# Hybrid SSD / DeltaNet layer on one core: merge-gate units woven into the chunk loop in steps of six matmuls

## The chip, the cores and the metric

The kernel runs on one core of a Trainium2 chip. The metric is the device time of one execution in microseconds (us), lower is better. Three runs of the kernel before gave 2930.74, 2930.89 and 2931.74 us; their median is 2930.89 us.

## The reference

One layer on x of 1024 tokens by 1024 channels, all in float32. What matters for the change:

```python
h = rms_norm(x, g_mix_pre)
z, xbc, dt_raw, qkv, gate, b_raw, a_raw, m_gate = split(h @ w_in)      # m_gate: 2048 columns
y_ssm = mamba2_branch(z, xbc, dt_raw, ...)      # recurrence over chunks
y_gdn = gdn_branch(qkv, gate, b_raw, a_raw, ...)  # recurrence over chunks, a triangular solve in each
gate_ssm, gate_gdn = split(sigmoid(m_gate))
mixed = gate_ssm * (y_ssm @ w_br_ssm) + gate_gdn * (y_gdn @ w_br_gdn)
x = x + rms_norm(mixed @ w_out, g_mix_post)
# then a gated conv-MLP (4096 wide) and a gated input embedding
```

The merge gate m_gate depends on h alone, and it is first used after both branches.

## The kernel before, in words

All activations are kept transposed: 128 channels on the partitions, 1024 tokens along the free dimension. A matrix product is cut into *units* of 128 output channels. A unit has 8 *steps*, one for each block of 128 input channels, and a step is six matmuls: two halves of 512 tokens, by high weights times high activations, high weights times low activations, low weights times high activations (`pe_steps`, lines 407, 410 and 411). GpSimd splits each unit's weights into high and low parts in `split_unit` (lines 392 and 394); a split of unit u waits until the unit before it has begun on TensorE (`unit_begun`), since there are two slots. SyncE loads the raw weights of two units in one block of 1 MB (`load_block`, line 369), and a block waits for the splits of the block two before it. The products are accumulated in PSUM, read by ScalarE (sigmoid or silu) or VectorE, and written ("spilled") to DRAM.

The stages, in order of time in the profile:

1. The convolution inputs, 36 units, each followed by four VectorE instructions (to about 512 us).
2. Stage A: the 16 units of z and gate, two for each of eight 128-token chunks. Between their steps TensorE does the DeltaNet preparation of a chunk: sums of squares (line 1024), transposed v (1031), Gram matrices (1009), transposed k (1043). The prepared tensors go to DRAM (`sp_a_stores`, lines 1148 to 1156), through SyncE's one queue, which also loads the next chunk (`sp_a_loads`, 1136 and 1141). The positions in the 16 steps of a chunk are 4, 8, 13 and 16.
3. The 16 merge-gate units, one after another (to about 952 us). Beside them VectorE inverts all 32x32 diagonal blocks by 63 dependent instructions (`dve_substitute`, lines 1189 to 1196); ScalarE stores them (line 1205).
4. The mixer: a loop over eight chunks, written as functions of one chunk for each engine (`pe_mixer`, `dve_mixer`, `act_mixer`, `pool_mixer`, `sp_mixer`). Nothing of it is issued before `ready_to_mix` holds on each engine, which asks for everything of stages 2 and 3. TensorE's order in `main` (line 749): two products with the DeltaNet state (710, "ks" and "qs"), the product with the SSM state (761, "off"), v_new (710), the intra-chunk product of one group of heads (742, `diag`), two products with v_new (710), `diag` of the other group, the state update (782), and then transposes and the block inverse of the next chunk. The matrix `dec` of 16 heads is loaded by a broadcast DMA (line 607) once `diag` has read the old one twice, then GpSimd subtracts and masks (669, 671), ScalarE takes the exponential (842), and VectorE multiplies by the scores (`mix_scores`, 913), which the next `diag` needs. VectorE writes the DeltaNet output behind it (`ygdn`, 984), and "off" waits for that.
5. The tail: branch projections, output projection, MLP and embedding; it first loads y from DRAM (line 1305).

The order within each engine's queue is that of the Python code; engines meet only through semaphores. The loops over chunks and units are hardware loops (`Fori`).

SBUF: `act_hi` and `act_lo`, the split activations (64 KB per partition), share their region with the mixer's buffers, so they are gone once the mixer begins.

Of the kernel before, what the change touches and what calls it, by code (L numbers as in the profile page):

```python
# [8 lines left out]
P = 128  # L9
# [25 lines left out]
def hybrid_block_kernel(nc, x, p, g_mix_pre, w_in, conv_ssm_w, conv_ssm_b, ssm_dt_bias, ssm_a_log, ssm_d, ssm_norm_g,  # L35
# [98 lines left out]
    zt = sb("zt", [P, KD, P], f32, ph2)  # L134
    gt = sb("gt", [P, KD, P], f32, ph2)
    dec = sb("dec", [P, SSM_HEADS, P], f32, ph2)
    bs = sb("bs", [P, 2 * SSM_GROUPS, P], f32, ph2)
    xc = sb("xc", [P, SSM_HEADS, SSM_HEAD_DIM], f32, ph2)
    xcd = sb("xcd", [P, SSM_HEADS, SSM_HEAD_DIM], f32, ph2)
    rinv = sb("rinv", [P, GDN_HEADS, P], f32, ph2)  # L140
    xinv = sb("xinv", [P, GDN_HEADS, P], f32, ph2)
    rhs = sb("rhs", [P, GDN_HEADS, P], f32, ph2)
    vnew = sb("vnew", [P, GDN_HEADS, P], f32, ph2)
    qs = sb("qs", [P, GDN_HEADS, P], f32, ph2)
    osq = sb("osq", [P, GDN_HEADS, P], f32, ph2)
    orst = sb("orst", [P, GDN_HEADS], f32, ph2)
    s_ssm = sb("s_ssm", [P, SSM_HEADS, SSM_HEAD_DIM], f32, ph2)
    s_gdn = sb("s_gdn", [P, GDN_HEADS, P], f32, ph2)
    ysum = sb("ysum", [P, D_MODEL], f32, ph2)
    xd = sb("xd", [P, KD, P], f32, ph2)  # L150
    yssm = sb("yssm", [P, KD, P], f32, ph2)
    ysq = sb("ysq", [P, KD, P], f32, ph2)
    yrs = sb("yrs", [P, SSM_GROUPS, P], f32, ph2)
    ygdn = sb("ygdn", [P, KD, P], f32, ph2)
    ph2.close()
    ph12.close()

# [83 lines left out]
    blocks_in, sub_step, d_kept = sem("blocks_in"), sem("sub_step"), sem("d_kept")  # L241
# [26 lines left out]
    def branch_weights(which, n):  # L268
# [25 lines left out]
    O_A = O_QKV2 + 4  # L294
    O_MG = O_A + 32
    O_BRS = O_MG + MG_T
    U_BRS = 1 + N_SPILL

# [3 lines left out]
            ("gdn", COL_QKV + 20 * P, 4, J_V + 4, O_QKV2), ("silu", COL_Z, Z_T, J_Z, O_A),  # L302
            ("silu", COL_GATE, GATE_T, J_GATE, O_A), ("sigmoid", COL_MG, 8, J_MG, O_MG),
            ("sigmoid", COL_MG + 8 * P, 4, J_MG + 8, O_MG + 8), ("sigmoid", COL_MG + 12 * P, 4, J_MG + 12, O_MG + 12)]
# [5 lines left out]
    def a_chunk(j0, n):  # L310
        return (0 if j0 == J_Z else 4) + n // 2

    def a_use(j0, n, it):

        b = A_BUF + n % 2
        return b, it * 2 + (O_A // NBUF + a_chunk(j0, n))

    def a_after(eng, s, it, c, per, more):

        eng.wait_ge(s, it * (2 * per) + (c * per + more + 1))  # L320
# [232 lines left out]
    def tokens(c, d=0):  # L553
        return slice((c + d) * P, (c + d + 1) * P) if isinstance(c, int) else ds(c * P + d * P, P)

    def chunk(c, d=0):
        return slice(c + d, c + d + 1) if isinstance(c, int) else ds(c + d, 1)
# [1681 lines left out]
```

## Time and profile before

| | us |
|---|---|
| median of three runs | 2930.89 |
| the profiled execution's own time | 2931.96 |
| span of the profile in that execution | 2929.4 |
| TensorE busy | 2631.1 (90%) |
| VectorE busy | 1395.2 (48%) |
| GpSimd busy | 1042.7 (36%) |
| ScalarE busy | 530.4 (18%) |

The profile's page divides the span into 40 slices of 73.2 us; a digit is the busy share in tenths. TensorE's digits fall to 5 to 7 in slices 14 to 19, which is the mixer. Times below are in us from the start of the span. In a timeline row the first number is the start, the second the length, then engine, line of the kernel, operation, output and inputs; in brackets stands the idle time in front of it and who ended it.

### The profile page before, as it was taken

The numbers are of one execution on the slowest core, as the hardware profiler recorded it, in microseconds if no ns is written. First come the engines' busy times: TensorE is split into PE (matmuls) and PEld (weight loads), VectorE is DVE, ScalarE is ACT, GpSimd is POOL, SyncE is SP. The second block draws the span as 40 slices with busy tenths as digits, with TensorE's granted clock in tenths as the row PEclk, the third lists the DMA queues.
The fourth block names the chain that finished last, engine by engine and source line by source line (L and its number), as shares of the span: only waits on it lengthen the run. The fifth ranks groups of instructions, "written<-read, shape, count | busy, mean of one in ns | idle before, by whom it ended". The sixth has DMA issues, their size and how long they took to land. (4 is left out here: it accounts for less than half of the span.)

```text
span 2929.4 us, 30007 instructions
## 1 busy us (share of the span) xinstructions
PE 2631.1 (90%) x11984; PEld 2129.1 (73%) x11984; DVE 1395.2 (48%) x1093; ACT 530.4 (18%) x530; POOL 1042.7 (36%) x549
## 2 busy tenths in 40 slices
PE   4999999899999667656999879999999999999995
PEld 3788887677787556554777658888888888888774
DVE  0679776212430455654133574444454444444664
ACT  3200111455310112222001320000000000000332
POOL 1233432465332343341325543333333333333361
PEclk8999999999999788887999989999999999999998
DMA  5122221787623655643333221111111111111231
GB/s 177 66 92 79 101 101 63 206 281 250 217 93 115 159 143 149 173 121 115 110 120 134 99 86 56 43 49 52 43 45 55 43 50 51 43 49 66 79 108 58
DMA packets 275592, 303.21 MB, mean 104 GB/s; under 512 B 43645, under 2 KB 241610, under 8 KB 271434
## 3 DMA queue, kind: packets, MB, share of 16 engines
q1 hardware_dynamic: 243280, 246.08, 27.4%
q10 hardware_dynamic: 32250, 56.28, 5.2%
q8 instruction: 42, 0.69, 0.1%
q14 instruction: 20, 0.16, 0.0%
HBM read 215.82 MB, written 86.51 MB: 103 GB/s over the span
## 5 line engine op out<-in xcount | busy, mean ns | idle before, releaser
L407 PE MATMUL ps<-act_hi,w_hi 128*128 128x512 f32 x2320 | 925.3, 399 | 40.0 <-DVE act_lo L1749 16.4
L411 PE MATMUL ps<-act_hi,w_lo 128*128 128x512 f32 x2320 | 916.8, 395 | 0.0
L410 PE MATMUL ps<-act_lo,w_hi 128*128 128x512 f32 x2320 | 911.0, 393 | 0.0
L392 POOL TENSOR_SCALAR w_hi<-w_raw 128x1024 fp32r<-128x1024 f32 x219 | 248.0, 1133 | 1491.9 <-PE ps L407 689.0
L394 POOL TENSOR_TENSOR w_lo<-w_raw,w_hi 128x1024 fp32r<-128x1024 f32 x219 | 574.9, 2625 | 18.3
L407 PEld LDWEIGHTS ps<-act_hi,w_hi 128*128 128x128 f32 x2320 | 437.5, 189 | 146.1 <-issue 27.8
L410 PEld LDWEIGHTS ps<-act_lo,w_hi 128*128 128x128 f32 x2320 | 437.7, 189 | 102.9 <-issue 2.2
L411 PEld LDWEIGHTS ps<-act_hi,w_lo 128*128 128x128 f32 x2320 | 437.1, 188 | 102.9
L1422 PE MATMUL ps<-f_hi,w_hi 128*128 128x512 f32 x480 | 189.1, 394 | 0.0
L1426 PE MATMUL ps<-f_hi,w_lo 128*128 128x512 f32 x480 | 188.2, 392 | 0.0
L1852 DVE TENSOR_TENSOR tile<-ps,tile 128x1024 f32<-128x1024 f32 x112 | 135.7, 1221 | 107.9 <-PE ps L1426 106.5
L2196 DVE SCALAR_TENSOR_TENSOR ring_a<-xin,par,ring_a 128x1024 f32<-128x1024 f32 x108 | 181.0, 1676 | 12.5 <-DVE ring_a L2196 1.6
L1425 PE MATMUL ps<-f_lo,w_hi 128*128 128x512 f32 x480 | 186.2, 388 | 0.0
L1640 ACT ACTIVATE fa<-fa 128x1024 f32<-128x1024 f32 x32 | 33.9, 1061 | 699.7 <-DVE fa L1831 699.7
L1396 PE MATMUL ps<-act_hi,w_hi 128*128 128x512 f32 x320 | 133.3, 416 | 23.6 <-DVE act_lo L1781 9.3
L1839 DVE TENSOR_TENSOR ring<-ps,fa 128x1024 f32<-128x1024 f32 x32 | 39.2, 1225 | 205.1 <-PE ps L411 203.9
L1825 DVE COPY xin<-ps 128x1024 f32<-128x1024 f32 x32 | 39.2, 1225 | 203.0 <-PE ps L411 199.5
L1400 PE MATMUL ps<-act_hi,w_lo 128*128 128x512 f32 x320 | 129.4, 404 | 0.0
L1399 PE MATMUL ps<-act_lo,w_hi 128*128 128x512 f32 x320 | 128.9, 403 | 0.0
L761 PE MATMUL ps<-s_ssm,xbc 128*128 128x512 f32 x32 | 27.7, 1016 | 102.8 <-DVE ygdn L984 102.8
L1426 PEld LDWEIGHTS ps<-f_hi,w_lo 128*128 128x128 f32 x480 | 90.1, 188 | 21.1
L1425 PEld LDWEIGHTS ps<-f_lo,w_hi 128*128 128x128 f32 x480 | 90.1, 188 | 20.2
(266 smaller groups left out, 2869.0 us busy)
## 6 DMA issues: line engine op xcount, KB each, us to landing
w_raw<-in_w_in_dram SPq DMA_DIRECT2D x34, 1024.0 KB, 5.3
spill<-ring_b ACTq DMA_DIRECT2D x68, 512.0 KB, 2.6
w_raw<-in_w_ffn_gate_dram SPq DMA_DIRECT2D x17, 1024.0 KB, 5.3
w_raw<-in_w_ffn_up_dram SPq DMA_DIRECT2D x17, 1024.0 KB, 5.4
w_raw<-in_w_ffn_down_dram SPq DMA_DIRECT2D x16, 1024.0 KB, 4.9
qkv_a<-spill SPq DMA_DIRECT2D x8, 1536.0 KB, 6.8
dec_a<-cum_rows SPq DMA_DIRECT2D x16, 512.0 KB, 12.6
gdn_in<-hrow SPq DMA_DIRECT2D x8, 1024.0 KB, 14.6
```

The source lines that it names most:

```text
L392: nc.gpsimd.tensor_scalar(hi, raw, 1.0, 0.0, ALU.mult, ALU.add).then_inc(split_done, 1)
L394: nc.gpsimd.tensor_tensor(lo, raw, hi.bitcast(f32), ALU.subtract).then_inc(split_done, 1)
L407: first = nc.tensor.matmul(o, wh, mov[0][:, k, c], start=(k == 0), stop=False)
L410: nc.tensor.matmul(o, wh, mov[1][:, k, c], start=False, stop=False)
L411: last = nc.tensor.matmul(o, wl, mov[0][:, k, c], start=False, stop=(k == KD - 1))
L1396: first = nc.tensor.matmul(dst, wh, mov[0][:, k, in_half(half)], start=(k == 0), stop=False)
L1400: last = nc.tensor.matmul(dst, wl, mov[0][:, k, in_half(half)], start=False, stop=(k == KD - 1))
L1422: first = nc.tensor.matmul(dst, wh[:, k, n * P:(n + 1) * P], mov_hi[:, k, c], start=(k == 0), stop=False)
L1425: nc.tensor.matmul(dst, wh[:, k, n * P:(n + 1) * P], mov_lo[:, k, c], start=False, stop=False)
L1426: last = nc.tensor.matmul(dst, wl[:, k, n * P:(n + 1) * P], mov_hi[:, k, c], start=False, stop=(k == 1))
L1852: v.tensor_tensor(tile3[:, j, :], buf(b), tile3[:, j, :], ALU.add).then_inc(tile_free[b], 1)
L2196: v.scalar_tensor_tensor(out=ring_a[:, slot, :], in0=xin[:, slot, tap:tap + SEQ], scalar=col_of(wname, tap * nt + t0 + n), in1=ring_a[:, s ...
```

## The change

- `act_hi`, `act_lo` and `ring_b` now live through the mixer. Room for them comes from: the wide table `tmh`, of which 128 columns a chunk are copied into `tmc` before stage A; `vnew` is written into `rhs`, `ygdn` into `gt`, `xd` into `yssm`, `osq` and `ysq` into one `sqs`, `yrs` into `sqs`, `xcd` into a half of `ring_b`. The new waits follow from that.
- Of the 16 merge-gate units, 3 stay ahead of the mixer; 13 (104 steps) are issued by `gemm` in `pe_mixer`: 8 steps in front of the first chunk, 12 in each chunk. All 13 use PSUM buffer 0, so each must be evicted (`mg_evict`) before the next begins.
- In `main`, `diag(c, 1)` goes ahead of the two products with v_new; on VectorE `ygdn` goes ahead of `mix_scores`.
- `dve_substitute` is cut into two halves of 128 rows: the first in stage A, in three pieces in chunks 4 to 6, the second behind stage A. `ready_to_mix` no longer asks for the stored inverse; that is waited for where it is needed.
- Stage A's DeltaNet work goes to steps 12, 15, 18, 21 of chunk 0 and 22, 26, 29, 32 of chunk 1.
- The hardware loops over stage A and over the mixer's chunks become straight-line code.

```diff
+    MG_PLAIN = 3
+    MG_MIX = MG_T - MG_PLAIN
@@ ready_to_mix
-        for i in range(2):
-            eng.wait_ge(spilled[i], 16 * (N_SPILL // 2))
         a_ended(eng)
-        eng.wait_ge(kept_bk, 16 * NCH + 1)
-        eng.wait_ge(d_kept, 16 * 8)
+        (kept_qk, kept_bk, kept_d, kept_n of all chunks)
+    def inverse_kept(eng):
+        eng.wait_ge(d_kept, 2 * 16 * 8)
@@ sp_mixer
+        def load_g(c):
+            inverse_kept(sp)
+            after(sp, yg_kept, c * 16)
+        blocks_at = {0: 4, 2: 5, 3: 6, 4: 7, 6: 8, 7: 9}
+        for c in range(NCH):
+            load_g(c)
+            load_qk(c + 1); load_xbc(c + 1); load_bv(c + 1)
+            if c in blocks_at:
+                block_load(blocks_at[c])
+            load_dec(c + 1); load_kd(c + 1); load_mq(c + 1); load_z(c + 1)
+            load_inv(c + 2)
@@ pool_mixer
+        split_unit(pool, U_MG, 0)
+        (memset nt, dd); ready_to_mix(pool); (memset s_ssm, s_gdn)
+        split_unit(pool, U_MG, 1)
+        decays(0)
+        split_unit(pool, U_MG, 2)
+        mg_split(0); decayed_x(0); mg_split(1)
+        for c in range(NCH):
+            states(c); skip_x(c)
+            if c % 2 == 0:
+                mg_split(3 * (c // 2) + 2)
+            elif c < NCH - 1:
+                mg_split(3 * (c // 2) + 4)
+            if c < NCH - 1:
+                decays(c + 1); decayed_x(c + 1)
+            if c % 2 == 0:
+                mg_split(3 * (c // 2) + 3)
@@ pe_mixer
+        def gemm(steps):
+            for _ in range(steps):
+                w, k = at[0] // KD, at[0] % KD
+                if k == 0:
+                    pe.wait_ge(tile_free[0], used_ahead(O_MIX, 0) + w)
+                    pe.wait_ge(split_done, 2 * (U_MIX + w) + 2)
+                pe_steps(pe, U_MIX + w, 0, range(k, k + 1), mov)
+                at[0] += 1
@@ main(c): the order after, gemm(n) new
+  ks, qs, off, gemm(2), v_new, diag 0, gemm(2), diag 1, ds, o, gemm(2), state,
+  invert_r, y transposes, gemm(2), x transposes, invert_h 0, scores, gemm(2),
+  sums of y squares, invert_h 1, gemm(1), invert_h 2, o transposes, gemm(1)
+  in front of chunk 0: invert_r, gemm(2), x transposes, invert_h 0, gemm(2),
+  scores, invert_h 1, gemm(2), invert_h 2, gemm(2)
@@ act_mixer
+            (v_new copies)
+            if c % 2:
+                mg_evict(3 * (c // 2) + 2)
+            (square of o, copy_r(c + 1))
+            if c % 2 == 0:
+                mg_evict(3 * (c // 2) + 1)
+            (square of y, copy_bs, Ln, Exp, exp_dec(c + 1), the two stores of y)
+            if c % 2:
+                mg_evict(3 * (c // 2) + 3)
+        in front of chunk 0: evict the 3 plain units; d_store(act, 1); ready_to_mix(act);
+        copy_r(0); copy_bs(0); exp_dec(0); mg_evict(0); inverse_kept(act)
@@ dve_mixer
-            mix_scores(c, 1) ahead of ygdn
+            ygdn into gt, then mix_scores(c + 1)
+        in front of chunk 0: scale_x, invert_x, mix_scores, inverse_kept(dve)
@@ pe_a
+    A_AT = [(12, 15, 18, 21), (22, 26, 29, 32)] + [(16 * c + 4, 16 * c + 8, 16 * c + 13, 16 * c + 16) for c in range(2, NCH)]
@@ dve_a
+        for at, i, row, n in TM_COLS:                       # 11 copies
+            v.tensor_copy(tmc[:, :, at:at + n], tmh[:, :, i, row:row + n]).then_inc(tm_kept, 1)
+            (after chunk c)
+            if 4 <= c < 7:
+                substitute(dve, 0, (0, 21, 42, SUB_STEPS)[c - 4:c - 2])
+        a_ended(dve)
+        dve.wait_ge(d_kept, 16 * 8)
+        substitute(dve, 1, (0, SUB_STEPS))
@@ sp_tail
+        sp.wait_ge(spilled[0], uses_spilled(J_MG + MG_PLAIN, 0) + 16 * MG_MIX)
```

Lines in parentheses or with a semicolon stand for longer code of the same content.

## Rows read from the trace of the kernel before

**Rows 1.** The page: busy tenths of TensorE in 40 slices.
```profile
PE   4999999899999667656999879999999999999995
```
**Rows 2.** Windows (length; busy us of PE, PEld, DVE, ACT, POOL; granted clock, DMA share, GB/s).
```profile
785.00:952.00 167.00, 166.43 (x714) 133.55 (x712) 47.37 (x63) 16.18 (x16) 53.25 (x30) 1.00 0.30 104
1134.00:1138.00 4.00, 3.03 (x4) 1.51 (x5) 3.93 (x7) 0.00 (x0) 0.53 (x1) 0.50 0.38 110
```
**Rows 3.** Timeline of one chunk on TensorE.
```profile
1134.97 3.75 PE L761 MATMUL ps<-s_ssm,xbc 128*128 128x512 f32 x4 [15.66 <-DVE ygdn L984]
1138.51 2.37 PE L710 MATMUL ps<-rhs,xinv 128*128 128x128 f32 x16
...
1147.86 1.88 PE L782 MATMUL ps<-xcd,bs 128*128 128x512 f32 x4
1149.58 1.95 PE L710 MATMUL ps<-dd,nt 128*128 128x128 f32 x16
...
1162.90 3.74 PE L710 MATMUL ps<-s_gdn,qk 128*128 128x128 f32 x32
1180.44 2.05 PE L761 MATMUL ps<-s_ssm,xbc 128*128 128x512 f32 x2 [13.80 <-DVE ygdn L984]
```
**Rows 4.** Timeline of the same chunk on the engines that prepare `dec`.
```profile
1148.05 0.37 SPq L607 DMA_DIRECT2D dec<-cum_rows  x1
...
1164.15 3.61 POOL L669 TENSOR_TENSOR dec<-dec,tmh 128x2048 f32<-128x2048 f32 x1 [23.35 <-DMA dec<-cum_rows]
...
1172.36 1.91 ACT L842 ACTIVATE dec<-dec 128x2048 f32<-128x2048 f32 x1 [11.75 <-POOL dec L671]
...
1174.30 4.80 DVE L913 TENSOR_TENSOR dec<-dec,bs 128x1024 f32<-128x1024 f32 x2 [10.05 <-ACT dec L842]
```
**Rows 5.** Timeline of ScalarE: two evictions of merge-gate units.
```profile
940.32 1.03 ACT L2126 ACTIVATE ring_b<-ps 128x1024 f32<-128x1024 f32 x1 [10.17 <-PE ps L411]
951.52 1.02 ACT L2126 ACTIVATE ring_b<-ps 128x1024 f32<-128x1024 f32 x1 [10.17 <-PE ps L411]
```
**Rows 6.** Timeline, TensorE and GpSimd, at the beginning of stage A.
```profile
523.05 6.34 PE L1024 MATMUL ps<-hrow,ones 128*128 128x512 f32 x8 [12.43 <-ACT hrow L1058]
...
536.56 0.50 PE L407 MATMUL ps<-act_hi,w_hi 128*128 128x512 f32 x1 [0.71 <-POOL w_lo L394]
...
528.65 1.90 POOL L1125 TENSOR_TENSOR dec_a<-dec_a,tmh 128x1024 f32<-128x1024 f32 x1 [30.53 <-DMA dec_a<-cum_rows]
```
**Rows 7.** Timeline, SyncE's and VectorE's side of chunks 0, 1 and 7 of stage A.
```profile
542.97 0.37 SPq L1136 DMA_DIRECT2D qkv_a<-spill  x1
...
569.95 1.23 DVE L1093 TENSOR_TENSOR ring_a<-ps,tmh 128x1024 f32<-128x1024 f32 x1 [16.22 <-DMA gdn_in<-ring_a]
...
770.01 1.23 DVE L1114 TENSOR_TENSOR ring_a<-ps,tmh 128x1024 f32<-128x1024 f32 x1 [3.90 <-PE ps L1043]
```
**Rows 8.** Issues from 500 to 1360: count, KB each, median us to landing.
```profile
gdn_in<-ring_a SPq DMA_DIRECT2D x8, 1024.0 KB, 10.2
dec<-cum_rows SPq DMA_DIRECT2D x8, 1024.0 KB, 16.7
```
**Rows 9.** Timeline: first and last v_new of the mixer, first load of y.
```profile
997.86 2.07 PE L710 MATMUL ps<-rhs,xinv 128*128 128x128 f32 x8 [5.87 <-DVE rhs L930]
...
1323.21 2.19 PE L710 MATMUL ps<-rhs,xinv 128*128 128x128 f32 x16
...
1353.59 20.90 SPq L1305 DMA_DIRECT2D ring<-y_cm  x8
```
**Rows 10.** Timeline: VectorE's inversion in stage 3, and GpSimd beside it.
```profile
786.47 2.47 DVE L1195 TENSOR_TENSOR dec_a<-dec_a,hrow 128x60 f32<-128x60 f32 x1
788.98 0.28 DVE L1193 TENSOR_TENSOR hrow<-dec_a 128x116 f32<-128x116 f32 x1
...
832.31 2.31 DVE L1196 COPY hrow<-dec_a 128x2048 f32<-128x2048 f32 x1
...
786.41 2.40 POOL L394 TENSOR_TENSOR w_lo<-w_raw,w_hi 128x1024 fp32r<-128x1024 f32 x1
```

More of the change, by code:

```diff
@@ L654, in sp_mixer @@
-        for c in range(NCH - 1):
-            loads(c, c < NCH - 2)
+                sp.dma_start(dd[r, :, r], d_c[c, :, b].rearrange("h i j -> i h j")).then_inc(in_d, 16)
+        ready_to_mix(sp)
+        sp.wait_ge(d_kept, 16 * 8)
+        for k in range(2):
+            sp.wait_ge(spilled[k], uses_spilled(J_MG, k))
+        sp.wait_ge(zeroed, 4)
+        load_dec(0)
+        load_xbc(0)
+        load_inv(0)
+        load_qk(0)
+        load_bv(0)
+        load_kd(0)
+        load_mq(0)
+        load_z(0)
@@ L708, in by_head @@
+        def by_head(pair, batch, lhs, rhs_of, done):
             for h in range(HA):
@@ L810, in main @@
             last.then_inc(ot_done, 1)
-        invert_r(0, 0)
-        x_rows_of(0, 0)
-        invert_h(0, 0, 0)
-        scores(0, 0)
-        invert_h(0, 0, 1)
-        invert_h(0, 0, 2)
-        after(pe, x_scaled, 1)
-        with pe.Fori(0, NCH - 1) as c:
-            main(c, True)
-        main(NCH - 1, False)
+            gemm(1)
+        ready_to_mix(pe)
+        pe.wait_ge(zeroed, 4)
+        for b in range(1, NBUF):
+            pe.wait_ge(tile_free[b], used_ahead(O_MIX, b))
+        invert_r(0)
+        gemm(2)
+        x_rows_of(0)
+        invert_h(0, 0)
+        gemm(2)
+        scores(0)
+        invert_h(0, 1)
+        gemm(2)
+        invert_h(0, 2)
+        gemm(2)
+        for c in range(NCH):
+            main(c, c < NCH - 1)
+        assert at[0] == KD * MG_MIX
+        for b in range(1, NBUF):
+            pe.sem_inc(tile_done[b], MG_MIX)
     def act_mixer(act):
@@ L875, in main @@
             after(act, yg_out, c + 1)
[L876 to L883 removed]
+            act.dma_start(y_c[:, KD:2 * KD, tokens(c)], gt[:, :, :]).then_inc(yg_kept, 16)
+            if c % 2:
+                mg_evict(3 * (c // 2) + 3)
+        for m in range(MG_PLAIN):
+            j = J_MG + m
+            b, count = uses(O_MG, m)
+            act.wait_ge(spilled[j % 2], 16 * (j // 2))
+            act.wait_ge(tile_done[b], count + 1)
+            a(ring_b[:, j % 2, :], buf(b), ACT.Sigmoid).then_inc(tile_free[b], 1)
+            act.wait_ge(tile_free[b], count + 1)
+            act.dma_start(spill[j], ring_b[:, j % 2, :]).then_inc(spilled[j % 2], 16)
+        d_store(act, 1)
+        ready_to_mix(act)
+        copy_r(0)
+        copy_bs(0)
+        exp_dec(0)
+        mg_evict(0)
+        inverse_kept(act)
+        for c in range(NCH):
+            main(c, c < NCH - 1)
+        after(act, yg_out, NCH)
+        for b in range(1, NBUF):
+            act.sem_inc(tile_free[b], MG_MIX)
     def dve_mixer(dve):
@@ new lines, in norms, with decays @@
+                a(flat(sqn_a[:, at:at + 8, :]), flat(sqn_a[:, at:at + 8, :]), ACT.Exp, scale=-0.5).then_inc(a_rs, 1)
+        def decays(c, nth):
+            i, at = c % 2, (8, 0)[nth]
+            after(act, a_seg, 4 * c + 2 * nth + 2)
+            a(dec_a[:, i, at:at + 8, :], dec_a[:, i, at:at + 8, :], ACT.Exp).then_inc(a_exp, 1)
+        evict(0)
+        squares(0)
+        for c in range(NCH):
+            norms(c)
+            decays(c, 0)
+            if c:
+                evict(2 * c)
+            decays(c, 1)
```

870 lines of the change are left out of this document (435 added, 435 removed).

## The prediction

> **What bounds the kernel now.** I read the page first: TensorE is busy nine tenths nearly everywhere, but only five to seven tenths in slices 14 to 19 [rows 1]. The windows tell the two stages apart. In the merge-gate stage TensorE is busy 166.43 of 167 us at clock 1.00; in the mixer a chunk opens at clock 0.50, the 1.2 GHz level, after TensorE stood idle [rows 2]. The timeline of a chunk shows why: "off" starts at 1134.97 and again at 1180.44, a period of 45.5 us, and in front of each TensorE has stood idle 13.8 to 15.7 us, waiting for `ygdn` [rows 3]. What is late there is `dec`: load issued 1148.05, GpSimd 1164.15, ScalarE 1172.36, VectorE 1174.30 plus 4.80, then `ygdn`, then "off" [rows 3, 4]. So the stage before the mixer is bound by TensorE, the mixer by the chain of `dec`. Moving work from the first into the holes of the second is worth its length as far as the holes hold it.
>
> **1. What leaves.** A merge-gate unit takes 951.52 - 940.32 = 11.2 us [rows 5], a step 1.4 us. Thirteen units are 145.6 us, and nothing else filled that stretch, so all of it leaves the time ahead of the mixer.
>
> **2. Stage A.** Copying the table costs 11 small instructions; at 0.28 us, the row of a 116-element one [rows 10], that is 3 us on VectorE ahead of the first load, which waited for the last spill for the same 3 us: nothing. The moved positions look as if they would fill the 12.43 us in front of the first sums [rows 6]. I doubt it. TensorE now runs unit 0 through (it began near 505, 18 us ahead of the sums: 5.6 us of steps and that idle time) to 516 and then needs the split of unit 1. In GpSimd's order that stands behind the subtraction of chunk 0, which waits for its load until 528.65; the split is ready at 536.5, when TensorE takes unit 1 in this trace too [rows 6], and the change leaves that order. Before, the sums and the v transposes were done by then; now they come after. The 15 units left at 536.5 with their share of preparation end near 770 [rows 7], so a chunk of two is 31.1 us, of which 22.4 are units; I estimate sums and v at 4.2 of the other 8.7. Restarting at the low clock costs about 2 (L761 takes 3.75 us at the low clock, the like L782 1.88 [rows 3]). Then chunk 1: from the load of the next q, k, v to the landing of the stored ring that VectorE waits for, the queue needs 569.95 - 542.97 = 27 us [rows 7]. With chunk 1 packed into 10 steps TensorE asks for that result after about 21 us; 5 are lost. Together stage A ends 11 us later. Bounds: 13 earlier (the idle time is all filled), 16 later. The first half of the inversion lies in VectorE's idle stretches of 14 to 16 us in chunks 4 to 6 (16.22 in front of L1093 [rows 7]), 21 small instructions in each: nothing; without that cover some 5 us a chunk.
>
> **3. From stage A to the first v_new.** Before, VectorE's last instruction of stage A ended at 771.2 [rows 7] and the first v_new began at 997.86 [rows 9]: 226.6 us. After, in order: the last ring store lands (10.2 [rows 8]); two memsets (1.9, an estimate by the like GpSimd rows); the load of `dec` (16.7 [rows 8]); subtraction and mask (1172.36 - 1164.15 = 8.2 [rows 4]); only then, in GpSimd's order, the split of plain unit 2 (3.5, two instructions, the longer 2.40 [rows 10]); unit 2 itself (11.2, and 1 for the clock, since TensorE waited some 13 us for that split); its eviction (1.0). The second half of the inverse is stored by ScalarE behind this eviction: eight issues, 4; then `copy_r` (1.2). Then TensorE alone: inverse products, scores, ks, qs and "off", 11.5 at the spacing of the like rows (16 matmuls 1.8, "off" 1.7 [rows 3]), and eight steps, 11.2. The sum is 10.2+1.9+16.7+8.2+3.5+12.2+1.0+4.0+1.2+22.7 = 81.6. VectorE's second half of the inversion ends well inside it: the whole ran from before 786.47 to 834.62 [rows 10], half of it is some 25 us. Gain 226.6 - 81.6 = 145.0 (this holds the 145.6 of part 1: the two plain-unit waits eat what the shorter load phase gives), less 11 of part 2: 134. Bounds: 155, if the load of `dec` and the plain units overlap wholly; 120, if the stores of the inverse land late.
>
> **4. The period of the chunks.** Before, (1323.21 - 997.86)/7 = 46.5 [rows 9]. Two floors now:
> - TensorE. From v_new at 1138.51 to the end of qs at 1166.64 is 28.1, less 0.5 idle and 0.4 of low clock at the start; "off" at full clock is 1149.58 - 1147.86 = 1.7 [rows 3]. That is 28.9; 12 steps are 16.8: 45.7 us with no gap at all. The clock should be full throughout.
> - The chain of `dec`: load 16.7, GpSimd 8.2, exponential 1.9, `mix_scores` 4.8 [rows 4, 8], then four instructions for `rhs` and two for `qs` on VectorE, 4.0 at their 0.68 us, `diag` 1.8, gemm(2) 2.8, `diag` 1.8: 42.0. It was longer before, since "off", v_new and two products stood in it; `diag(c,1)` moved forward and `ygdn` out of it pay for the step pair put in.
>
> TensorE is the bound, by little. I followed one chunk through all engines from "off" at 0: v_new 4.5, `diag` 6.3 and 10.9, sums of y squares 32.6, o transposes 39.5, next "off" 45.4. VectorE is free of `ygdn` at 42.8 and ends `mix_scores` at 47.6, `rhs` at 50.4, so v_new of the second half and `diag` wait about half a us. Evictions: units end after the fourth gemm (26.3; sigmoid with its table load is done at 28.7, the next unit asks at 29.8), or after the second, or at the chunk's end, where exponential, two stores and the eviction end about 0.8 us before the step that needs the buffer. GpSimd has 18.2 us of its own and 1.6 splits of 3.5: 24 of 46. The stored `ygdn` must land before `gt` is loaded; that is early in the chunk, the load needed late. One in-place reuse (`rhs`) waits for the products with v_new, long done. What I can't place is small: waits between engines that used to lie in the idle time, 1 MB of weights in front of the `dec` load in six chunks. I take 47.5. Bounds: 45.4 (every gap closed) and 54 (the `dec` load slowed by a whole block and its chain with it).
>
> VectorE may be slowed further. An instruction of 60 elements took 2.47 us where the next, of 116, took 0.28, and it ended with GpSimd's L394 of 2.40 us [rows 10]; how often the two meet in the chunks no row shows. In the forecast this is part of the 47.5; it is rival R5. The Trainium skill (GPSIMD Engine Reference, "1. Specifications") says that GpSimd's SBUF interfaces are shared with VectorE, which is held up where it reads two SBUF inputs. By that rule the added splits hit `rhs` and `mix_scores`, and the row agrees with it.
>
> Seven periods: 7 x (47.5 - 46.5) = 7 us lost.
>
> **5. The end.** From the last v_new to the first load of y was 30.4 us [rows 9], most of it waits between VectorE, ScalarE and TensorE. Nine steps now fall ahead of the last transposes, 12.6 us, of which the waits hide the most (y squares 23.7 after v_new, output 31.8), but the load now waits also for the spill of the last gate unit: evicted and stored behind the two y stores, at 38.5. 8 us lost; bounds 3 and 14.
>
> **Sum.** Against the profiled execution's own 2931.96: -134 + 7 + 8 = -119, so 2813. The median is 1.1 below that execution: 2812.
>
> **The rivals.**
> - *R1, the holes do not take it.* The chain stays in front and waits of other engines add up: period 52 to 54. For it: both floors are within 4 us, and 16.7 is a slow load that grows under traffic. Against: 4 us of slack in front of `mix_scores`. 7 x 6 more: about 2855.
> - *R2, better handovers.* Stage A gains its 12 idle us instead of losing 11, or the load phase in front of the mixer is shorter, and the period is 46: about 2780. For it: 12.43 of idle time are there [rows 6]. Against: the split order.
> - *R3, slower than before.* The load of `dec` is held in SyncE's queue. It now stands behind the loads of `gt`, `qk`, `xbc`, `bv` and the weight block; each has its own wait, the block's on a split which waits for a step of TensorE. The period is the chain's 42.0 plus the time by which the load is issued after `diag` ends. If the block's wait is met only in the last third of the chunk, near 38 instead of 12.7, that is 67.3: 7 x 20.8 = 146 lost, and 2931.96 - 134 + 146 + 8 = 2952. It is slower than before from an issue after 35, a period of 64.5. Against: for every block the split it needs comes at least a third of a chunk earlier by the order above.
> - *R4, the move does nothing:* the steps only stretch the chain as it stands, 46.5 + 16.8 = 63.3 a chunk, 7 x 16.8 = 118 lost: 2924. Against: only one pair stands between `mix_scores` and the next load.
> - *R5, VectorE held by GpSimd.* Each of the 1.6 new splits a chunk holds an instruction on the path for one GpSimd instruction, 2.4 us: 3.8 more, period 51.3, 2839. For it: the 2.47 us row. Against: VectorE is on the path for some 8 us of a chunk only.
>
> **How the numbers follow.** Forecast (period 46 to 50) 0.58, R1 0.12, R2 0.13, R5 0.10, R3 0.02, R4 0.02, anything else (half of it above the range) 0.03. Likeliest 2812; its own range, from the bounds of parts 2 to 5 taken not all at one end, 2795 to 2833. For 8 in 10 I go from 2785 to 2855. A change is told from none beyond 0.2%, some 6 us. Faster 0.96, same 0.01, slower 0.03.
>
> **What would show it.** In the new profile: three units between stage A and the mixer, with TensorE idle in front of the second and longer in front of the third (part 3); a first idle time in stage A of some 20 us after unit 0 (part 2); clock 0.95 or more in the chunks; distance of "off" 46 to 49, with no wait over 2 us on `ygdn`; the load of `dec` issued within 15 us of "off". A period over 52 with GpSimd waiting for the load is R1; the load's issue after 25 us is R3. I am wrong if v_new of chunk 0 begins outside 855 to 880, or the period lies outside 45 to 50.

## The result, and the profile after

2819.26 us, median of 4 runs (2814.93 to 2823.72), against 2931.31 beside it: ratio 0.9616 [0.9605, 0.9628], 3.8% faster. The forecast was 2812, range 2785 to 2855. The profiled execution is the one of 2814.93 us; its span is 2813.2 (before 2929.4) at a mean granted clock of 0.969 (before 0.951). So 116.2 us of span went.

Line numbers moved: v_new is now a L765 (was L710), "off" L817 (L761), the last instruction of a stage A chunk L1244 (L1114), the split of weights L403 and L405 (L394), steps L418 to L422. First the page of the changed kernel, TensorE's busy tenths, the answer to [rows 1]: the hole in the middle is gone.

```profile
PE   4999999799979999979899699999999999999995
```

Windows of the changed kernel (columns as in [rows 2]): stage A's end to the first v_new, an even chunk, an odd chunk, all chunks.

```profile
795.00:876.00 81.00, 65.02 (x314) 53.25 (x313) 51.08 (x80) 12.02 (x12) 31.39 (x17) 0.89 0.59 178
876.00:921.00 45.00, 45.00 (x304) 39.58 (x302) 25.21 (x25) 11.91 (x15) 24.61 (x11) 1.00 0.60 170
921.00:968.00 47.00, 45.71 (x303) 39.98 (x303) 30.05 (x34) 15.51 (x18) 23.56 (x10) 1.00 0.62 173
876.00:1198.00 322.00, 317.41 (x2116) 278.21 (x2114) 194.46 (x198) 94.15 (x114) 171.42 (x71) 1.00 0.65 182
```

In the chunks TensorE is busy 317.4 of 322 us at clock 1.00, the 2.4 GHz level; before, a window from the first to the last v_new (998 to 1323) had 218.3 busy of 325 at 0.83. TensorE has become the bound there. The timeline of the changed kernel gives the borders of the stretches: the last instruction of stage A, first "off" and v_new, last "off", last v_new, the first load of y (answers to [rows 7, 9]).

```profile
793.98 1.23 DVE L1244 TENSOR_TENSOR ring_a<-ps,tmc 128x1024 f32<-128x1024 f32 x1 [3.78 <-PE ps L1139]
...
871.58 1.88 PE L817 MATMUL ps<-s_ssm,xbc 128*128 128x512 f32 x4
876.10 1.95 PE L765 MATMUL ps<-rhs,xinv 128*128 128x128 f32 x16
...
1193.49 1.88 PE L817 MATMUL ps<-s_ssm,xbc 128*128 128x512 f32 x4
1198.29 1.16 PE L765 MATMUL ps<-rhs,xinv 128*128 128x128 f32 x8
...
1237.38 0.81 SPq L1463 DMA_DIRECT2D ring<-y_cm  x2
```

| stretch | before | after | difference | forecast |
|---|---|---|---|---|
| stage A ends (L1114, L1244) | 771.2 | 795.2 | +24.0 | +11 |
| from there to the first v_new | 226.6 | 80.9 | -145.7 | -145.0 |
| first to last v_new, 7 periods | 325.4 | 322.2 | -3.2 | +7 |
| last v_new to the first y load | 30.4 | 39.1 | +8.7 | +8 |
| sum | | | -116.2 | -119 |

The total of this execution is 3 us off, but two terms are off by 13 and 10 in opposite directions, so part of the agreement is luck. The median is 7 us above the forecast of 2812; the profiled execution is the fastest of the four, 4.3 below the median.

**Stage A.** Timeline of TensorE and GpSimd at its beginning:

```profile
517.59 0.77 PE L418 MATMUL ps<-act_hi,w_hi 128*128 128x512 f32 x1 [12.41 <-POOL w_lo L405]
536.02 0.76 PE L418 MATMUL ps<-act_hi,w_hi 128*128 128x512 f32 x1 [5.08 <-POOL w_lo L405]
576.09 0.48 PE L418 MATMUL ps<-act_hi,w_hi 128*128 128x512 f32 x1 [4.06 <-POOL w_lo L405]
...
513.97 1.05 POOL L403 TENSOR_SCALAR w_hi<-w_raw 128x1024 fp32r<-128x1024 f32 x1 [26.89 <-DVE tmc L1218]
```

Unit 0 itself waited 12.4 us: GpSimd's split for it stands behind the wait for the copied table. Each of the three waits is for a split by GpSimd. The splits of unit 1 (536.02) and of unit 3 (576.09) stand behind GpSimd's subtractions of chunks 0 and 1, which began at 528.09 and 568.13, when their loads had landed. The second k transposes begin at 593.32, 10.9 later than before (582.39). Chunks 2 to 4 are 31.07 us, as predicted. The other 13 us come later, where VectorE computes pieces of the first half of the inversion. The timeline of VectorE in the second piece, and of GpSimd beside it:

```profile
725.66 0.39 DVE L1354 TENSOR_TENSOR sub_d<-sub_d,xin 128x220 f32<-128x220 f32 x1
726.08 1.97 DVE L1351 TENSOR_TENSOR xin<-sub_n,sub_d 128x228 f32<-128x228 f32 x1
728.09 2.46 DVE L1354 TENSOR_TENSOR sub_d<-sub_d,xin 128x228 f32<-128x228 f32 x1
...
731.73 2.47 DVE L1354 TENSOR_TENSOR sub_d<-sub_d,xin 128x234 f32<-128x234 f32 x1
...
738.79 0.41 DVE L1351 TENSOR_TENSOR xin<-sub_n,sub_d 128x240 f32<-128x240 f32 x1
...
725.83 1.97 POOL L1262 TENSOR_TENSOR dec_a<-dec_a,tmc 128x1024 f32<-128x1024 f32 x1 [8.89 <-DMA dec_a<-cum_rows]
727.88 2.41 POOL L1264 TENSOR_TENSOR dec_a<-dec_a,m_strict 128x1024 f32<-128x1024 f32 x1
...
731.53 2.41 POOL L405 TENSOR_TENSOR w_lo<-w_raw,w_hi 128x1024 fp32r<-128x1024 f32 x1
```

Read the starts side by side: each VectorE instruction that begins with one of GpSimd's takes as long as that one, 1.97 to 2.47 us in these rows, where a like one alone takes 0.39 to 0.41. Below, this is called a hold. Six of the 21 instructions of this piece are held, 12.5 us together. The piece runs from 724.83 to 744.0, 19 us in a hole of 14 to 16, and chunk 6 is 36.7 us long instead of 31.1.

### The profile page after: what moved, and what is told of

Read it like the earlier page. It is cut to its first block and busy times, and to the rows that moved or that the text cites. A ratio compares the mean times of both kernels' runs of the same rounds, so it can differ in the third digit from the quotient of the medians.

```text
span 2813.2 us, 29393 instructions
## 1 busy us (share of the span) xinstructions
PE 2619.8 (93%) x11984; PEld 2122.6 (75%) x11984; DVE 1436.1 (51%) x1167; ACT 538.8 (19%) x536; POOL 1048.1 (37%) x549
## 5 line engine op out<-in xcount | busy, mean ns | idle before, releaser
L418 PE MATMUL ps<-act_hi,w_hi 128*128 128x512 f32 x2320 | 940.1, 405 | 71.7 <-POOL w_lo L405 35.5
L422 PE MATMUL ps<-act_hi,w_lo 128*128 128x512 f32 x2320 | 919.2, 396 | 0.0
L403 POOL TENSOR_SCALAR w_hi<-w_raw 128x1024 fp32r<-128x1024 f32 x219 | 247.1, 1129 | 1431.1 <-PE ps L418 603.9
L405 POOL TENSOR_TENSOR w_lo<-w_raw,w_hi 128x1024 fp32r<-128x1024 f32 x219 | 573.6, 2619 | 18.3
L418 PEld LDWEIGHTS ps<-act_hi,w_hi 128*128 128x128 f32 x2320 | 440.7, 190 | 179.4 <-issue 64.9
L422 PEld LDWEIGHTS ps<-act_hi,w_lo 128*128 128x128 f32 x2320 | 439.5, 189 | 105.3
L2317 DVE SCALAR_TENSOR_TENSOR ring_a<-xin,par,ring_a 128x1024 f32<-128x1024 f32 x108 | 180.9, 1675 | 12.5 <-DVE ring_a L2317 1.6
L1554 PE MATMUL ps<-act_hi,w_hi 128*128 128x512 f32 x320 | 133.0, 416 | 23.8 <-DVE act_lo L1939 9.2
L1997 DVE TENSOR_TENSOR ring<-ps,fa 128x1024 f32<-128x1024 f32 x32 | 39.2, 1225 | 205.1 <-PE ps L422 203.8
L1983 DVE COPY xin<-ps 128x1024 f32<-128x1024 f32 x32 | 39.2, 1225 | 203.0 <-PE ps L422 199.5
L1580 PEld LDWEIGHTS ps<-f_hi,w_hi 128*128 128x128 f32 x480 | 90.2, 188 | 17.9
## 6 DMA issues: line engine op xcount, KB each, us to landing
dec_a<-cum_rows SPq DMA_DIRECT2D x16, 512.0 KB, 12.7
```

What stands on the lines that cost most here:

```text
L403: nc.gpsimd.tensor_scalar(hi, raw, 1.0, 0.0, ALU.mult, ALU.add).then_inc(split_done, 1)
L405: nc.gpsimd.tensor_tensor(lo, raw, hi.bitcast(f32), ALU.subtract).then_inc(split_done, 1)
L418: first = nc.tensor.matmul(o, wh, mov[0][:, k, c], start=(k == 0), stop=False)
L422: last = nc.tensor.matmul(o, wl, mov[0][:, k, c], start=False, stop=(k == KD - 1))
L1554: first = nc.tensor.matmul(dst, wh, mov[0][:, k, in_half(half)], start=(k == 0), stop=False)
L1580: first = nc.tensor.matmul(dst, wh[:, k, n * P:(n + 1) * P], mov_hi[:, k, c], start=(k == 0), stop=False)
```

## The experiments

Each starts from the changed kernel unless said otherwise. Stretches are read from each kernel's own trace; medians from runs beside the kernel before.

**e1: the first half of the inversion left out.**
```
+            if m == 0 and 2 <= step < SUB_STEPS - 1:
+                dve.sem_inc(sub_step, 1)
+                dve.wait_ge(sub_step, SUB_STEPS * m + step + 1)
+                continue
```


> The changed kernel, but of the first half of the inversion (chunks 4 to 6 of stage A) only the copies and the ones on the diagonal are computed; steps 2 to 61 are left out, so the inverse of half of the blocks is wrong. Theory A (VectorE's pieces, slowed by GpSimd, hold chunks 5 to 7 of stage A up): the last VectorE instruction of stage A ends 13 us earlier, at about 782 instead of 795.2; chunks 5 to 7 are 31.1 us each like chunks 2 to 4; time about 2819 - 13 = 2806. Rival B (the late end comes from stores or loads of the queue in these chunks, not from the arithmetic): the end stays within 3 us of 795, time 2816 to 2819.

Measured: 2804.99 us, ratio 0.9585 [0.9560, 0.9609]. Stage A ends at 782.9 (-12.3), chunks 5 to 7 are 31.5, 31.1 and 31.1. Theory A.

**e9: VectorE's pieces as they are, GpSimd's instructions beside them cut to 8 columns (chunks 5 to 7).**
```
-            split_unit(pool, U_A, m)
+            split_unit(pool, U_A, m, part=8 if m >= 10 else None)
...
+            w = 8 if m >= 10 else P
+            d = d[:, :, 0:w]
```


> The changed kernel, but in chunks 5 to 7 of stage A GpSimd's splits, subtractions and masks touch only 8 of their 128 columns, so the products of these units and the decays of these chunks are wrong; VectorE's pieces of the inversion are as in the changed kernel. Theory A (GpSimd's instructions hold VectorE's): the second and third piece take 10 to 12 us instead of 19 and 18, no instruction of theirs above 1 us, and chunks 6 and 7 are 31.1 us long instead of 36.7 and 33.5; chunk 5, whose piece waits for its load, stays at 36; stage A ends 8 us earlier, time 2811. Rival B (the pieces are long by themselves, by their own reads of two operands, or through the DMA traffic): the pieces and chunks as before, 2819.

Timeline of VectorE and GpSimd in the second piece of this kernel:

```profile
723.68 0.40 DVE L1355 TENSOR_TENSOR xin<-sub_n,sub_d 128x234 f32<-128x234 f32 x1
724.12 0.51 DVE L1358 TENSOR_TENSOR sub_d<-sub_d,xin 128x234 f32<-128x234 f32 x1
724.66 0.41 DVE L1355 TENSOR_TENSOR xin<-sub_n,sub_d 128x238 f32<-128x238 f32 x1
...
724.07 0.30 POOL L1266 TENSOR_TENSOR dec_a<-dec_a,tmc 128x64 f32<-128x64 f32 x1 [10.90 <-DMA dec_a<-cum_rows]
```

No instruction of the piece is over 0.51 us, the piece takes 9 us (721.57 to 730.8) instead of 19, and chunks 5 to 7 are 32.2, 31.0 and 31.1. Stage A ends at 783.8, 11.4 earlier. This shows the holds to be the cause of 11.4 of the 12.3 us that leaving VectorE's arithmetic out (e1) gains. One miss: chunk 5 fell too, from 36.1 to 32.2, though its piece began only 0.7 us earlier (698.59 for 699.30). So the late load alone costs that chunk 1.1 us, and holds in a piece that begins late make up most of the rest. The four times scatter from 2803 to 2834 (0.9610 [0.9562, 0.9658]), so the median says little; the trace decides.

**e6: the load of the inversion's blocks issued earlier.**
```
+            if c == 4:
+                blocks_load(0)
             block_load(c + 1)
             if c < NCH - 1:
                 loads(c + 1)
-            if c == 4:
-                blocks_load(0)
```


> The changed kernel, but the load of the blocks for the first half of the inversion is issued ahead of the loads of chunk 5 instead of behind them. Theory A (the first piece begins 10.5 us late because its load waits behind 5.75 us of broadcast issues, and so holds chunk 5 up by 5 us; the other pieces are held by GpSimd): the first piece begins within 2 us of the end of chunk 4's ring (688.8) instead of at 699.3, chunk 5 falls from 36.1 to 31.1 us, chunks 6 and 7 stay at 36 and 33, time about 2814. Rival B (the wait for the load is hidden in the wait for v): chunk 5 as before, time 2819. If the scatter of the changed kernel's times (8.8 us) comes from this load, the times of this kernel scatter by less than 5 us.

Measured: 2816.45, 0.9603 [0.9590, 0.9616], no difference that can be told; the times spread over 6.6 us, where I had expected under 5 if this load made the scatter. The piece did begin at 690.5 with no wait, and then met GpSimd:

```profile
690.51 2.27 DVE L1341 COPY sub_d<-sub_n 128x1024 f32<-128x1024 f32 x1
...
693.00 2.12 DVE L1351 TENSOR_TENSOR xin<-sub_n,sub_d 128x30 f32<-128x30 f32 x1
...
696.14 2.42 DVE L1351 TENSOR_TENSOR xin<-sub_n,sub_d 128x58 f32<-128x58 f32 x1
```

Beside the copy, six instructions of the piece are held now, where one was when it began late. Chunk 5 stayed at 35.6. A wait was traded for holds; that the load's wait by itself explains chunk 5 is refuted.

**e2: the first three splits ahead of the table's wait.**
```
+        for m in range(3):
+            split_unit(pool, U_A, m)
         pool.wait_ge(tm_kept, len(TM_COLS))
...
-            split_unit(pool, U_A, m)
+            if m == 2:
+                split_unit(pool, U_A, 3)
+            elif m > 3:
+                split_unit(pool, U_A, m)
```


> The changed kernel, but GpSimd splits the weights of the first three units of stage A before it waits for the copied table and before its first subtraction. Theory A (the order on GpSimd holds TensorE's units 0 to 2, 12.4, 5.1 and 4.1 us): TensorE begins unit 0 near 505 instead of 517.6 and runs three units through; after that the chain from the sums to the stored ring sets chunk 1, so k_rows of chunk 1 comes about 10 us earlier than 593.3 (582 to 585); time about 2809. Rival B (the chain of loads, squares and stores sets the start anyway, and the units only wait elsewhere): k_rows of chunk 1 within 3 us of 593, time 2816 to 2819. Rival C (all the idle time goes): 20 us earlier, 2799.

Measured: 2804.24, 0.9576 [0.9561, 0.9591]. TensorE runs through to the first sums:

```profile
526.90 3.75 PE L1112 MATMUL ps<-hrow,ones 128*128 128x512 f32 x4 [5.15 <-ACT hrow L1174]
...
544.33 0.77 PE L418 MATMUL ps<-act_hi,w_hi 128*128 128x512 f32 x1 [4.21 <-POOL w_lo L405]
...
582.83 1.04 PE L1139 MATMUL ps<-ident,hrow 128*128 128x128 f32 x8
```

The second k transposes come 10.5 earlier (582.83), as theory A had it. One wait for a split is left, 4.21 us in front of unit 3. Stage A ends 15.7 earlier (779.5); the other 5 are chunks 5 and 6, which lost 1.2 and 4.1 where they had lost 5.0 and 5.7; the pieces meet GpSimd at other places, but that this is the reason was not tried.

**e3: no weave, all thirteen units ahead of the first chunk** (their evictions, splits and loads too).
```
-            for _ in range(steps):
+            for _ in range(KD * MG_MIX if at[0] == 0 else 0):
...
-        mg_evict(0)
+        for w in range(MG_MIX):
+            mg_evict(w)
```


> The changed kernel, but all thirteen units are computed ahead of the first chunk, and the loop holds only the chunks in their new order. Theory A (the new order of diag and ygdn made the chain of dec shorter; the weave itself is bound by TensorE): period of the chunks by the starts of off 42 to 43.5, against 46.5 in the kernel before and 46.0 woven; TensorE idle 13 to 15 us in each chunk. Rival B (the chain is as long as before and the woven steps lie in it by chance): 45.5 to 46.5. Time: 13 units of 11.2 plus some 2 us each for evictions with one pair of banks, in place of 7 x 3 us: about 2819 + 13 x 13 - 25 = 2963 by A, 2985 by B; slower than the kernel before by A too.

Measured: 2939.86, 1.0032 [1.0019, 1.0045]. "Off" from 1055.98 to 1317.86 in six periods: 43.6 us, and v_new gives 43.4 over seven. Without the weave a chunk is 3 us shorter than before (46.5). The new order of the products is the likely reason, but e3 keeps every other change of the loop too, and they were not tried apart. TensorE is idle 10.5 us a chunk (199.1 busy of 261.9 in the six periods, at a mean granted clock of 0.88), less than the 13 to 15 of theory A.

The prediction's floor of 42.0 for this chain contains 2.8 us of woven steps. Without them it is 39.2, so e3's chunk is some 4 us above it; 0.9 to 1.9 of that are GpSimd's two instructions on `dec`, 9.1 to 10.1 us for the 8.2 of the sum; the rest was not followed up. That TensorE and not this chain bounds the woven chunk is shown by the window of the even chunk above, busy 45.00 of 45 us, and not by e3.

Against e3 the changed kernel is 2939.9 - 2819.3 = 120.6 faster. Not all of it is the weave's: the thirteen units in a row share one pair of banks and take 12.64 us each instead of 11.2, which is 19 us that two pairs would not cost. My estimate of the time was 23 too high: a unit costs 1.4 us more, not 2, and I had not taken off the eight steps (11.2) that the changed kernel has ahead of chunk 0.

**e4: the second split of an even chunk done in the odd chunk.**
```
-            elif c < NCH - 1:
-                mg_split(3 * (c // 2) + 4)
+            else:
+                mg_split(3 * (c // 2) + 3)
+                if c < NCH - 1:
+                    mg_split(3 * (c // 2) + 4)
...
-            if c % 2 == 0:
-                mg_split(3 * (c // 2) + 3)
```


> The changed kernel, but the split that GpSimd does at the end of even chunks is done behind skip_x of the odd chunk that follows. Theory A (this split beside mix_scores and rhs makes the odd chunks 2 us longer): mix_scores takes 2.4 us instead of 3.3 to 5.3 at every chunk, odd periods fall from 47.0 to 45.1, 3 or 4 of them in the seven, time 2819 - 7 = 2812. Rival B (odd chunks are longer by another cause, an eviction or a weight load): periods stay 45.0 and 47.0, time 2819. Rival C (the split now comes too late for the unit that needs it at the third pair of steps): 2 us or more lost in odd chunks with TensorE waiting for w_lo, 2825.

In the changed kernel "off" starts at 871.58, 916.53, 963.55, 1009.26, 1056.37, 1101.32, 1148.41 and 1193.49: even chunks 45.0 to 45.1 (one 45.7), odd ones 47. The timeline of VectorE, GpSimd and TensorE at the end of chunk 0 and the beginning of chunk 1, of the changed kernel, and then of VectorE and TensorE in e4:

```profile
914.10 2.35 POOL L405 TENSOR_TENSOR w_lo<-w_raw,w_hi 128x1024 fp32r<-128x1024 f32 x1
914.23 5.28 DVE L1011 TENSOR_TENSOR dec<-dec,bs 128x1024 f32<-128x1024 f32 x2
...
920.37 2.35 POOL L716 TENSOR_TENSOR s_ssm<-s_ssm,tmc 128x1024 f32<-128x1024 f32 x1
...
921.59 1.67 DVE L1028 TENSOR_TENSOR rhs<-bv,rhs 128x512 f32<-128x512 f32 x1
...
923.32 1.16 PE L765 MATMUL ps<-rhs,xinv 128*128 128x128 f32 x8 [1.15 <-DVE rhs L1028]
```
```profile
920.13 2.34 DVE L1011 TENSOR_TENSOR dec<-dec,bs 128x1024 f32<-128x1024 f32 x2
...
924.55 0.81 DVE L1028 TENSOR_TENSOR rhs<-bv,rhs 128x512 f32<-128x512 f32 x1
...
926.64 1.95 PE L765 MATMUL ps<-rhs,xinv 128*128 128x128 f32 x16
```

`mix_scores` falls from 5.3 to 2.34 us, `rhs` from 1.67 to 0.81, and v_new is one stretch without a wait. (1195.20 - 877.05)/7 = 45.45 against 45.99: 3.8 us in the seven periods and 3.4 more from the last "off" on. Measured: 2811.98, 0.9591 [0.9579, 0.9604], -7.3: theory A in the mechanism, though this profiled run's own stage A ended 5.7 later than the changed kernel's. One part missed: the odd chunks fell to 45.4 on the average, not 45.1, and the even ones rose to 45.5. In five of these chunks, where it was one in the changed kernel, TensorE waits 0.25 to 0.82 us for `qs` (L1069) in front of the o transposes; why was not tried.

**e5: plain unit 2 split ahead of `dec`'s subtraction.**
```
-        decays(0)
         split_unit(pool, U_MG, 2)
+        decays(0)
```


> The changed kernel, but GpSimd splits plain unit 2 ahead of the subtraction and mask of dec instead of behind them. Theory A (TensorE's 12.4 us of idle time there are not on the path, because VectorE's second half of the inversion ends at 842.6, and its store and copy_r follow on ScalarE): the idle time in front of unit 2 goes, unit 2 ends 12 us earlier, but from the end of stage A to the first v_new only 3 to 4 us are gained, 77 instead of 80.9; time about 2816. Rival B (the sum of the prediction's part 3, in which the split and unit 2 stand on the path): 12 us gained, first v_new 69 after stage A's end, time 2807. Rival C: the split beside VectorE's second half lengthens it, nothing gained or a loss, 2819 to 2822.

The idle time of 12.43 in front of plain unit 2 (830.52 in the changed kernel) went, and 13.06 stand in front of the second product, for ScalarE:

```profile
830.29 1.02 ACT L967 ACTIVATE ring_b<-ps 128x1024 f32<-128x1024 f32 x1 [10.18 <-PE ps L422]
...
843.92 1.75 ACTq L1362 DMA_DIRECT2D d_dram<-sub_d  x4
845.70 1.88 ACTq L1362 DMA_DIRECT2D d_dram<-xin  x4
848.06 1.08 ACT L914 ACTIVATE rinv<-ps 128x512 f32<-128x512 f32 x2 [16.75 <-issue]
```

Stage A's end to v_new is 77.6 (was 80.9), -3.3: theory A, the path runs over VectorE's second half and its store. The median, 2813.03, 0.9586 [0.9571, 0.9601], is 6 below, more than the stretch explains; that is within the scatter.

**e7: e2, e4, e5 and e6 together.**

> The changed kernel with four edits together: the first three splits of stage A ahead of the table's wait, the split at the end of even chunks behind skip_x of the next, plain unit 2's split ahead of dec's subtraction, and the load of the blocks ahead of chunk 5's loads. Measured alone against the changed kernel's 2819.3: the first gave 15.0 and the second 7.3; expected of the other two: 3 and 5. They lie in different stretches. Theory A: they add up, 2789 (2785 to 2794); end of stage A near 775, first v_new 77 later, chunks 45.4 each. Rival B: the first edit has already given what the load of the blocks would give (its chunk 5 fell to 32.3 us without it), 2794.

Measured: 2799.86, 0.9539 [0.9524, 0.9553], five runs from 2791 to 2820; 11 above the sum by A. 5 of them are e6's, which gave nothing. The trace agrees with the sum behind stage A (77.6 us to the first v_new, periods of 45.2), not in it: stage A ends at 786.8, where I had 775. The second k transposes begin at 586.59, 3.8 later than in e2, and chunks 5 to 7 are 33.9, 37.2 and 33.7, each with a piece of six holds. The profiled run was the slowest, by a delay in the last stages (last section).

**e8: e7, the first woven unit whole ahead of the first product, and other cuts.**
```
+        gemm(8)
         invert_r(0)
-        gemm(2)
...
-                substitute(dve, 0, (0, 21, 42, SUB_STEPS)[c - 4:c - 2])
+                substitute(dve, 0, (0, 25, 39, SUB_STEPS)[c - 4:c - 2])
```


> As the kernel with the four edits, and two more: the first woven unit is computed as a whole ahead of the first product of chunk 0's inverse, in TensorE's idle time, instead of in four pairs between the products; and the first half of the inversion is cut at steps 25 and 39 instead of 21 and 42. Theory A: between VectorE's second half and the first v_new 22.7 us of TensorE had 11.2 of steps in them; without them the products wait for VectorE and ScalarE instead, 6 us are gained; the middle piece, in which the products have most elements, shrinks, and chunks 6 and 7 lose 4 us less together: time 10 below the kernel with four edits, about 2779. Rival B (the first woven unit's split, behind dec's subtraction, comes so late that unit 0 ends after VectorE's second half): 0 to 3 us lost there, 2785 to 2792.

Measured: 2784.48, 0.9501 [0.9488, 0.9515]. Stage A's end to v_new is 68.6, 9.0 less than in e7 (77.6), where I expected 6. The cuts gained nothing, where I expected 4: chunks 5 to 7 are 37.3, 31.1 and 36.5, 104.8 together as in e7. Each of the three pieces has six held instructions, 12.3 to 12.5 us; the piece of 14 steps is 16.2 us long and free, those of 25 and 24 steps are 22.3 and 19.1 us long and are not.

**e11: as e8, with five pieces.**
```
+                substitute(dve, 0, ((0, 16), (24, 38), (46, SUB_STEPS))[c - 4])
...
+            if 5 <= c < 7:
+                substitute(dve, 0, ((16, 24), (38, 46))[c - 5])
```


> As the kernel with four edits and the first woven unit ahead (2784.5 us), but the first half of the inversion in five pieces: 16 steps behind chunk 4, 8 ahead of chunk 5's gram, 14 behind it, 8 ahead of chunk 6's gram, 17 behind it. Theory A (in the kernel before this one a piece of 14 steps cost its chunk nothing, 31.07, and pieces of 25 and 24 steps 6.2 and 5.4 us; the stretch of 14 to 16 us holds some 16 steps with GpSimd beside them, and the 4 to 5 us ahead of gram hold 8): chunks 5 to 7 are 31.1 to 32.5 each, 9 to 11 us gained, time 2775. Rival B (the stretch ahead of gram is not free, since GpSimd's holds lengthen these steps too): each of the two costs 3 to 5 us, 2780 to 2785.

Measured: 2775.58, 0.9451 [0.9425, 0.9477]. Chunks 5 to 7 are 31.5, 31.1 and 31.1, stage A ends at 772.2. Theory A. That the median agrees within 1 us is partly luck, since the six times spread over 9 us. The 8 steps ahead of chunk 6's gram took 6.05 us with two holds and still cost the chunk nothing.

**e12: as e11, and the wait for the last spill behind the loads of y.**
```
-        sp.wait_ge(spilled[0], uses_spilled(J_MG + MG_PLAIN, 0) + 16 * MG_MIX)
...
+                if i == 0:
+                    sp.wait_ge(spilled[0], uses_spilled(J_MG + MG_PLAIN, 0) + 16 * MG_MIX)
```


> As the kernel with five pieces, but SyncE's wait for the last gate unit's spill stands ahead of the first load of a gate instead of ahead of the first load of y. Theory A (the end of the prediction's part 5: in the changed kernel the spill was issued at 1234.71 and the y load at 1237.38, 6.0 us after the store of gt was issued at 1231.37; stores of that kind land in 4.5): the y load is issued about 1.5 us earlier, time 1 to 2 us below the kernel with five pieces. Rival B (what is late in the end is the chain of ygdn itself, with the steps in front of its transposes): nothing gained.

Measured: 2774.19, 0.9455 [0.9426, 0.9484]; against e11 not to be told apart by time. In the traces the store of `gt` to the load of y is 5.5 us in e11 (1192.50 to 1197.98) and 3.8 in e12 (1191.49 to 1195.26), 1.7 less. This is the fastest median here, 45 us below the changed kernel.

**e10: the changed kernel again.**

> The changed kernel as it is, to see how its times and stretches scatter. Theory A (the scatter has two sources: GpSimd's instructions meet VectorE's pieces differently from run to run, and in some runs all matmuls after about 1500 us are 2% further apart, 233 instead of 229 ns, as in the profiled run of the kernel with four edits, which adds 19 us): median 2816 to 2821, stage A ends between 793 and 801 in the profiled run, and the times lie either within 9 us of each other or some 20 us above. Rival B (the scatter lies in the chunks of the mixer): stage A ends within 1 us of 795.2 and the period of the chunks lies outside 45.5 to 46.5.

Measured: 2817.44 (2806.59 to 2824.38), 0.9604 [0.9579, 0.9630]. Its trace has stage A's end at 795.7 and a period of 46.14, much like the first. The six times spread over 18 us without two groups, and its profiled run (2814.86) is not one of the far ones: neither theory is shown, though the median and the end of stage A lie where A had them.

## Why the prediction was right, and where not

- **What bounds, and what becomes the bound (right).** The chunks were bound by the chain of `dec` and had room for 12 steps; now TensorE is busy 45.0 of 45 us in an even chunk. The floor of the chain was too low: e3 has 43.6 us without the woven steps, where the sum without them is 39.2.
- **Parts 1 and 3, the units that leave and the way to the first v_new (right by sum, partly by luck).** 80.9 against 81.6. The path is not the one I added up: e5 took my wait for the split and unit 2 out and gained 3.3, not 12. Two chains end within 4 us of each other, and I took VectorE's second half of the inversion as 25 us; it took 40 (802.73 to 842.6): seven of its 63 instructions were held, 17.6 us together, and the others come to the 22 that are left. e8 shows that the 11.2 us of steps, which I let stand in the sum, were 9.0 of path.
- **Part 2, stage A (wrong, +24.0 for +11).** The step that failed is "The first half of the inversion lies in VectorE's idle stretches ...: nothing". It cost 12.3 us (e1), by GpSimd's hold (e9). I had the row of it, 2.47 us for 60 elements [rows 10], and charged it to the chunks of the mixer alone. The 10.9 at the beginning match my 11, but only half of my reasons held. Unit 1 began at 536.02, behind the subtraction, as I had it (536.5). I had unit 0 run through to 516, and it began at 517.59, because I passed over the new wait in front of GpSimd's first split; so the idle time of some 20 us behind unit 0 did not come. That wait cost nothing by itself, since unit 0 was through at 530.9, 5.08 us before unit 1 could begin. And the 5 us that I charged to the store's chain did not come: TensorE waited 4.06 us for the split of unit 3 instead. e2 takes three splits out of the way of both and gives the beginning back: 582.8 is where the kernel before had it (582.4). It does not price them one by one.
- **Part 4, the period (right within its bounds, too high by 1.5).** 46.0 for 47.5. TensorE's own work was 45.0, not 45.7. Even chunks take that; odd ones take 2 more. That is R5's mechanism at a smaller price: e4, which moves one of the splits, gives back 0.5 us a chunk of the 1.0 above TensorE's time, and R5 had 3.8. R1, R3 and R4 did not come: the load of `dec` was issued 12.9 us after "off" in chunk 0 (884.45), where I said 12.7.
- **Part 5, the end (right).** 8.7 for 8. e12 shows 1.7 of it to be the wait for the spill; the rest is the steps ahead of the last transposes, which was not tried alone.
- The Trainium skill (GPSIMD Engine Reference, "1. Specifications") says GpSimd shares its SBUF interfaces with VectorE, with contention for instructions with two SBUF inputs. Here the traces agree: VectorE's instructions with two SBUF inputs took 2.0 to 2.5 us beside GpSimd's of 128x1024 elements, and 0.4 alone. A copy with one input was held too (last section).

## What to carry to other kernels

Work moved into VectorE's idle time is dearer than its own length where GpSimd works beside it: count GpSimd's instructions in the hole, and as an estimate give each one its full duration on VectorE (six of them made 9 us into 19 here). An idle time that is taken away shows up as the next chain's wait (e5, e6), so ask which chain ends second before pricing it. And where a new wait is put in front of a queue's first element, look for what stands behind it that did not need it.

## What the hardware showed that I had not expected

- A small VectorE instruction with two operands in SBUF takes the whole duration of a GpSimd instruction that begins with it: 0.4 us become 2.0 to 2.5, and in e8 even 3.70 and 4.71 beside the subtraction and mask of `dec` (timeline of VectorE and GpSimd in e8):

```profile
805.51 0.41 DVE L1356 TENSOR_TENSOR sub_d<-sub_d,xin 128x234 f32<-128x234 f32 x1
805.95 3.70 DVE L1353 TENSOR_TENSOR xin<-sub_n,sub_d 128x238 f32<-128x238 f32 x1
809.68 4.71 DVE L1356 TENSOR_TENSOR sub_d<-sub_d,xin 128x238 f32<-128x238 f32 x1
...
805.66 3.72 POOL L691 TENSOR_TENSOR dec<-dec,tmc 128x2048 f32<-128x2048 f32 x1 [7.54 <-DMA dec<-cum_rows]
809.46 4.67 POOL L693 TENSOR_TENSOR dec<-dec,m_incl 128x2048 f32<-128x2048 f32 x1
```

- The hold goes both ways, and it is not only for two operands. This is the first copy of chunk 5's piece in the changed kernel, a VectorE instruction with one input in SBUF, with GpSimd's subtraction and mask beside it:

```profile
699.30 2.18 DVE L1341 COPY sub_d<-sub_n 128x1024 f32<-128x1024 f32 x1 [10.49 <-DMA sub_n<-nb_dram]
...
698.58 1.90 POOL L1262 TENSOR_TENSOR dec_a<-dec_a,tmc 128x1024 f32<-128x1024 f32 x1
700.56 3.17 POOL L1264 TENSOR_TENSOR dec_a<-dec_a,m_incl 128x1024 f32<-128x1024 f32 x1
```

  The copy began inside the subtraction and took 2.18 us, where it takes 1.12 in e9; the mask began inside the copy and took 3.17, where those of the second piece take 2.41 and 2.46. In both, the one that began second ends about its own length after the first has ended.

- In the profiled run of e7 all matmuls of the last stages stood further apart at the same granted clock. The same window of the changed kernel and of e7:

```profile
1900.00:2500.00 600.00, 600.00 (x2623) 492.34 (x2622) 270.70 (x180) 38.25 (x36) 197.32 (x109) 1.00 0.16 49
```
```profile
1900.00:2500.00 600.00, 600.00 (x2573) 486.02 (x2572) 266.58 (x179) 38.21 (x36) 190.93 (x106) 1.00 0.15 47
```

  2623 matmuls against 2573, 1.9%. From the first load of y to the end the run takes 1599.8 us (1218.21 to 2818.0), where the changed kernel takes 1575.8, so this adds 24 us to its 2819.70; the others of the kernel have 2791 to 2803. No other trace here shows it. What spreads the other times of the changed kernel over 18 us stays open.
